# A two-layer hybrid encoder in fp32 on one core: the sum of squares behind the transposes, and four projection products one to a step

## What is computed

```python
h = layer_norm(x, ln_in_g, ln_in_b)
for l in range(DEPTH):                       # 2 layers
    proj = h @ w_in[l]
    ...                                      # split into the inputs of four groups of 256 channels
    out_a = windowed_gqa_sink(...)           # 4 heads, window of 128, ALiBi, sink
    out_b = short_conv_mixer(...)
    out_c = fourier_mixer(...)
    out_d = dense_gqa_blocks(...)            # 4 heads, all 512 keys, after RMS norm and rotary
    mix = jnp.concatenate([rms_norm(o, g[i * 256:(i + 1) * 256])
                           for i, o in enumerate((out_a, out_b, out_c, out_d))], axis=-1)
    h = layer_norm(DN_ALPHA * h + mix @ w_out[l], ln1_g[l], ln1_b[l])
    ffn = jnp.square(jax.nn.relu(h @ w1[l])) @ w2[l]
    h = layer_norm(DN_ALPHA * h + ffn, ln2_g[l], ln2_b[l])
```

## Time and profile before

| | |
|---|---|
| median of 3 runs | 1057.16 us (1056.75 to 1057.83) |
| the profiled execution | 1057.18 us, span of its instructions 1055.1 us |
| TensorE busy | 1038.5 us, 98% of the span |
| VectorE, ScalarE, POOL busy | 72%, 50%, 11% |
| mean granted clock of TensorE | 0.998 of full |
| steps 11 to 14 in layer one | 161.26 to 180.67 us |
| chain that ended last | 94% on TensorE |

### The profile page before, as it was taken

The page is one execution under the profiler, slowest core; times in us unless marked ns, Lnnn a source line. Parts: engine busy times, 40 slices in busy tenths (PEclk is TensorE's granted clock), DMA queues, the critical chain, the costliest instruction groups (busy, mean ns, idle before and its releaser), DMA issues.

```text
span 1055.1 us, 15201 instructions
## 1 busy us (share of the span) xinstructions
PE 1038.5 (98%) x5281; PEld 868.7 (82%) x5281; DVE 761.5 (72%) x1035; ACT 532.4 (50%) x777; POOL 116.8 (11%) x122
## 2 busy tenths in 40 slices
PE   7999999999999999999999999999999999999996
PEld 6888887988888888888888888879888888888885
DVE  7845876878668757758887558677884884785787
ACT  3433666665355255355634247666634643642654
POOL 5200343200000000000002004331000000000003
PEclk9999999999999999999999999999999999999999
DMA  8432023031521521521243410311243134125122
GB/s 292 160 120 80 1 61 121 9 121 59 187 74 40 199 80 40 174 106 53 108 144 139 160 41 22 120 42 49 80 157 122 40 124 156 40 92 186 40 80 80
DMA packets 17378, 105.47 MB, mean 100 GB/s; under 512 B 2016, under 2 KB 2704, under 8 KB 5792
## 3 DMA queue, kind: packets, MB, share of 16 engines
q1 hardware_dynamic: 15984, 98.70, 26.3%
q0 software_dynamic: 1184, 5.86, 1.7%
q10 hardware_dynamic: 144, 0.07, 0.0%
HBM read 101.49 MB, written 2.10 MB: 98 GB/s over the span
## 4 chain that ended last, share of the span: by engine, by line
PE 94%; POOL 2%; issue 1%; ACT 1%; DMA 1%; DVE 0%; DVEq 0%; SPq 0%; POOLq 0%; ACTq 0%
PE bank L465 19%; PE bank L466 18%; PE bank L467 18%; PE bank L815 9%; PE bank L814 9%; PE bank L813 9%; PE bank L753 2%; PE bank L738 2%; PE bank L474 1%; PE bank L644 1%; PE bank L645 1%; POOL w_lo L1816 1%; PE bank L541 1%; POOL x L1911 1%; PE bank L548 1%
## 5 line engine op out<-in xcount | busy, mean ns | idle before, releaser
L465 PE MATMUL bank<-h_hi,w_hi 128*128 128x512 f32 (+1 forms) x688 | 257.8, 375 | 0.0
L466 PE MATMUL bank<-h_lo,w_hi 128*128 128x512 f32 (+1 forms) x688 | 257.5, 374 | 0.0
L467 PE MATMUL bank<-h_hi,w_lo 128*128 128x512 f32 (+1 forms) x688 | 257.5, 374 | 0.0
L813 PE MATMUL bank<-w_hi,hid_hi 128*128 128x512 f32 x448 | 174.4, 389 | 0.0
L815 PE MATMUL bank<-w_hi,hid_lo 128*128 128x512 f32 x448 | 174.3, 389 | 0.0
L814 PE MATMUL bank<-w_lo,hid_hi 128*128 128x512 f32 x448 | 174.3, 389 | 0.0
L1257 DVE TENSOR_TENSOR w_lo<-w_raw,w_hi 128x2048 fp32r<-128x2048 f32 x62 | 141.8, 2287 | 39.2 <-ACT w_hi L929 32.7
L929 ACT CAST w_hi<-w_raw 128x2048 fp32r<-128x2048 f32 x56 | 107.1, 1913 | 85.8 <-PE bank L815 61.5
L466 PEld LDWEIGHTS bank<-h_lo,w_hi 128*128 128x128 f32 x688 | 129.5, 188 | 23.1
L465 PEld LDWEIGHTS bank<-h_hi,w_hi 128*128 128x128 f32 x688 | 129.5, 188 | 23.0
L467 PEld LDWEIGHTS bank<-h_hi,w_lo 128*128 128x128 f32 x688 | 129.5, 188 | 23.1
(11 more groups left out here) (184 smaller groups left out, 1610.3 us busy)
## 6 DMA issues: line engine op xcount, KB each, us to landing
w_raw<-in_weights SPq DMA_DIRECT2D x63, 1024.0 KB, 4.7
w_third<-in_weights SPq DMA_DIRECT2D x23, 1024.0 KB, 4.8
rows<-in_rows POOLq DMA_DIRECT2D x4, 1024.0 KB, 4.7
w_raw<-in_weights SPq DMA_DIRECT2D x4, 512.0 KB, 8.5
out_h<-x SPq DMA_DIRECT2D x8, 256.0 KB, 2.0
x<-in_x SPq DMA_DIRECT2D x3, 512.0 KB, 9.6
dft<-in_dft SPq DMA_DIRECT2D x2, 512.0 KB, 7.0
qk_gain<-in_qk_gain POOLq DMA_DIRECT2D x3, 192.0 KB, 3.5
```

The costliest lines, as they stand in the source:

```text
L465: pe.matmul(dst, s_hi, m_hi, start=first, stop=False)
L466: pe.matmul(dst, s_hi, m_lo, start=False, stop=False)
L467: return pe.matmul(dst, s_lo, m_hi, start=False, stop=last)
L813: pe.matmul(bank[dst + t][:], s_hi, m_hi, start=start, stop=False, skip_group_check=goes_on)
```

## The change

Two things, both in the attention stage:

- In an even step TensorE's sum of squares of a quad (`sum_quad`) stands behind the transposes of the step (`turn_probs`) and not ahead of them.
- The four products (2, 3, 0), (2, 3, 1), (3, 0, 0), (3, 0, 1) stood two in step 11 and two in step 13. Now they stand one in each of the steps 11, 12, 13 and 14. The order of the items is the same, and so are their banks. VectorE takes them in the same steps.

ScalarE's and POOL's lists are not changed.

```diff
 for _g in range(3):
-    SIDE_STEPS.update({4 * _g + _t: w_items(_g, _t, _t + 1) for _t in range(TOK)})
+    SIDE_STEPS.update({4 * _g + _t: w_items(_g, _t, _t + 1) for _t in range(TOK) if (_g, _t) != (2, 3)})
 SIDE_STEPS[3] = [("s", 1)] + SIDE_STEPS[3]
-SIDE_STEPS.update({13: w_items(3, 0, 1), 15: w_items(3, 1, 2), 16: w_items(3, 2, 4)})
+SIDE_STEPS.update({11: [("w", 2, 3, 0)], 12: [("w", 2, 3, 1)], 13: [("w", 3, 0, 0)], 14: [("w", 3, 0, 1)],
+                   15: w_items(3, 1, 2), 16: w_items(3, 2, 4)})
...
                     if quad_scaled_in(p) is not None:
                         turn_inverse(quad_scaled_in(p))
+                    for u in pair(p - 1):
+                        turn_probs(u)
                     if quad_high_in(p) is not None:
                         sum_quad(quad_high_in(p))
-                    for u in pair(p - 1):
-                        turn_probs(u)
```

## The result

| | before | changed |
|---|---|---|
| median on the same chip | 1057.12 us (1056.75 to 1057.83, 4 runs) | 1063.63 us (1061.86 to 1063.88, 4 runs) |
| profiled execution | 1057.18 us, span 1055.1 | 1063.62 us, span 1061.8 |

The ratio is 1.0057, with a 95% interval of 1.004 to 1.0075: slower by about half a per cent. The forecast was 1059.9 us and the range ended at 1061.6, so the time lies outside. Among the experiments one execution, of the kernel with both queues reordered, was slow (1758.19 us at a mean granted clock of 0.557) and is left out of the ratios.

A forecast was written before the change was run, and what follows sets the result against it. TensorE bounds the kernel, busy 1038.5 of 1055.1 us. Steps 11 to 14 go from 19.41 to 20.73 us, +1.32 per layer, +2.64 in two, +2.7 with the swap: 1059.9 us, range 1058.1 to 1061.6.

The forecast's parts named there:

- Steps 11 to 13 and the wait of step 12: TensorE, each layer: steps of 5.43, 3.35 and 5.46 us, step 12's wait for `head_square` gone, 2.28 us gained.
- POOL's chain in step 14: Product (3, 0, 1) now in step 14: POOL's `rstd` power starts at S14 + 4.85, sum at + 5.87, TensorE idle at least 2.7 us.
- Two engines on one memory: Step 14: VectorE's centring delays POOL's addition on `head_square`; sum at S14 + 6.24, step 6.49 us, 0.37 us per layer.
- rival 1: Step 14: POOL's addition not delayed by VectorE, step takes 6.12 us, +0.95 per layer, 1059.2 us; chance 0.18.
- What comes behind the stall: From step 15 on: nothing takes the loss back and VectorE's work adds nothing, so zero us.
- rival 5: TensorE's clock falls through the stall of step 14: 6.8 us per layer, 1073 us; chance 0.03.
- The swap: Sum of squares behind the transposes: +0.01 us per even step 4 to 10, 0.1 us in eight, ends -0.2 and +0.9.
- Rival 3: Steps 12 and 14: POOL's power doesn't delay the sum, both waits gone, 1.82 us less per layer, 1053.5 us; chance 0.07.

The follow-up runs named there:

- The filled stall: The changed kernel plus 22 identity transposes on TensorE between the transposes and the sum of step 14, results unused: 1059.73 us.
- the first order tried: The changed kernel with POOL's power for tile 0's `rstd` moved behind the `head_square` addition and the copy of the next inverse: 1056.51 us.
- the better one: The changed kernel with POOL's `rstd` power directly behind the `head_square` addition for quads 5 and 6, ahead of the inverse's copy: 1055.85 us.
- the best kernel: The changed kernel with POOL's power behind its addition, VectorE's `mix_lo` and scaling ahead of row statistics, and the sum ahead of the transposes again: 1053.23 us.

## Why the prediction was wrong, point by point

- **Steps 11 to 13 and the wait of step 12: right.** 5.43, 3.40 and 5.43 us against 5.43, 3.35 and 5.46; the sum at S12 + 3.26 against + 3.18, without a wait.
- **POOL's chain in step 14: right.** The power for `rstd` started at S14 + 4.73 against + 4.85, released by `var_eps`, as the diff and POOL's queue said.
- **Two engines on one memory: right.** Power 0.70, addition 0.66, sum at S14 + 6.12 against + 6.24. Holding VectorE back gave S14 + 5.75 against the 5.87 of rival 1. That the power, too, would be stretched (0.55 to 0.70) was not in the sum. It changed nothing there, since by the rows the addition's end goes by the first half of the centring, and that ended at S14 + 5.75 (182.10) in place of + 5.92. The addition ended 0.31 us behind it, where the sum had 0.27.
- **What comes behind the stall, put at nothing: the step that failed.** The sum had +1.32 per layer, then "Nothing behind takes that back", and ended there. Measured are +1.21 and +1.24, and then +1.58 and +1.60 that it had as rival 5, the fall of the clock, at a chance of 0.03. The filled stall shows that this is all of the difference behind step 15. The argument against rival 5 was a clock of 1.00 still 3.8 us behind the last work at the program's end. Those rows end one window too early. The next two of the same trace are:

```profile
1051.00:1052.00 1.00, 0.00 (x0) 0.00 (x0) 0.79 (x2) 0.00 (x0) 0.02 (x1) 0.72 0.63 240
1052.00:1053.00 1.00, 0.00 (x0) 0.00 (x0) 0.62 (x1) 0.00 (x0) 0.00 (x0) 0.50 0.25 92
```

So the kernel before shows the fall itself, at about 1051.4, 4.3 us behind the end of TensorE's last record. One such distance says little: at the end of the changed kernel's program it is 2.9 us (1053.91 to about 1056.76), with the swap alone 2.0 (1047.59 to about 1049.54), with the table alone 5.3 (1053.89 to about 1059.23). In the stall of the changed kernel it was 3.2 us behind the transposes' last record in layer one (178.74 + 1.03, to about 182.95) and 3.7 in layer two (700.45 + 1.03, to about 705.19), when TensorE had already been back for 0.5 and 1.0 us. A single row at 3.8 us could not rule the rival out. The sentence on the Trainium skill in rival 5 (TensorE: Matmul & The Clock Gate, "What's actually happening", an idle array at half its clock) had the direction right. The trace differs in the moment: the array was at work again when its clock was halved.

- **Rival 5's price was wrong as well.** It was 6.8 us per layer, for a whole step at half the clock. The clock came back after 3.4 us (about 182.95 to 186.36), and 1.6 us were lost. With that price the case would have given 1059.9 + 3.2 = 1063.1 us, 0.5 short of the result.
- **The swap: mis-sized.** The sum had +0.01 us per even step, measured are 0.06 to 0.07: S4 to S11 is 34.92 against 34.66 over four of them, 0.5 us in all. Behind the transposes the two operations take 1.01 us (169.91 to 170.92), ahead of them 0.96. The 0.80 was the distance from transposes to scores. From transposes to the sum it is 0.87 (169.91 to 170.78). The upper end of the term, 0.9 us, held it.
- **Rival 3, faster at 1053.5 if POOL's order allowed it: right in its step, wrong in its time.** Steps 11 to 14 shrank to 17.67 us as it said, but two thirds came back behind S15 with POOL's queue in the first order tried, and 0.8 of 1.74 us with the better one, since `mix_lo` of quad 5 stood behind tile 0's statistics on VectorE and was in no list of waits before. Only with VectorE's queue in order and the swap undone did the time get there, 1053.23.

Left open: what makes the start differ by 0.56 us, which no part of the change reaches. Why the clock falls in one execution and not in the next, at the same stall, is not shown either. The varying distances above, 2.0 to 5.3 us between the end of work and the fall, fit with it: a fall that comes early finds the stall, one that would come late finds TensorE at work for long again. That is an inference, and no run tests it. Open is also whether stalls between 0.65 us (those of the kernel before, behind which it stayed at 1.00) and 1.71 us can bring it down.

## What to carry to other kernels

A stall of TensorE of 2 to 3 us can cost more than its own length: here each fall of the clock cost another 1.6 us, in the work behind the stall, where no wait is listed and the engine looks 100% busy. It fell in nearly every execution at 2.69 us and in some at 2.33 and 1.71. So read the granted clock for some microseconds behind each long wait, and compare durations of equal matmuls. And when a row is to show that something does not happen, read on until it does: here it happened in the next row.

Before taking a wait away, look for the second chain that ends at the same place: an operand whose writer finishes within a few tenths of a microsecond of its reader is a wait that isn't shown yet, and here it ate the whole gain of the swap.

A table that moves work between steps has to be checked against each in-order queue that waits for the moved result. Here one power of 0.55 us ahead of a short addition cost 7.4 us over the two layers by the stages (S4 to H, 75.74 against 72.02 us in layer one), the fall of the clock included, twice the 3.7 us by which the best kernel beats the one before.

## What the runs showed of the hardware that was not expected

- The granted clock fell to 0.50 after stalls of 2.69, 3.57, 2.33 and 1.71 us, the last two (and by its length one execution at 2.69) not in every layer of every execution. In the changed kernel it did so after the stall was over, and stayed there for 3.4 us of full work. Between the end of TensorE's work and the fall lay anything from 2.0 to 5.3 us at the ends of the programs, 4.3 in the kernel before.
- Transposes of the identity kept the clock at 1.00: 22 of them, with 0.29 us of idle time left, in the profiled execution, and all seven have a mean clock of 0.997 or more against 0.994 to 0.996 in the changed kernel's four.
- POOL's operations mostly got slower beside VectorE's with two operands: a power on one column from 0.55 to 0.70 or 0.99 us, an addition of 128 columns from 0.45 to 0.66, a copy of 256 columns to 0.83 and 0.85. In the best kernel, where power and centring start within 0.02 us of each other, the power kept its 0.55. VectorE paid a little: in the changed kernel the two halves of the centring took 1.58 us in place of 1.52, and the two of the scaling 1.54 in place of 1.41.
